# A two-layer hybrid trunk: twelve held expert units with a place each, other PSUM banks for value products and the last scan levels, and the first expert product inside the second gather half

## The reference

```python
def hier_moe(h, wg, bg, we, be, w1, w3, w2):     # 32 experts, 4 groups of 8, 2 experts per token
    gprob = softmax(t @ wg + bg); gidx = top-1 group
    eprob = softmax(logits of that group's 8 experts); top-2, renormalised
    gate = weight of each (token, expert), 0 for most
    for e in range(32):
        he = silu(t @ w1[e]) * (t @ w3[e])
        y = y + gate[:, e:e+1] * (he @ w2[e])
x = x + even_mixer(rmsnorm(x)); x = x + hier_moe(rmsnorm(x))     # layer 0
x = x + odd_mixer(rmsnorm(x));  x = x + hier_moe(rmsnorm(x))     # layer 1
```

## Time and profile before

| what | value |
|---|---|
| runs | 1302.06 us median (1301.33, 1302.06, 1309.36) |
| profiled execution | 1305.92 us, span of its core 1304.1 us |
| PE busy | 1143.5 us (88% of the span), of which the modelled ends are a part |
| DVE, ACT busy | 359.7 us (28%), 217.0 us (17%) |
| DMA | 459.10 MB, mean 352 GB/s |
| granted TensorE clock, mean | 0.973 of full speed |

### The profile page before, as it was taken

How to read it: one execution, slowest core, us unless ns; L and a number is a source line. 1 busy time by engine, 2 the same in 40 slices (tenths; PEclk the granted TensorE clock), 3 DMA queues, 4 the chain that set the end, 5 groups by cost and what they waited for, 6 DMA issues and landing times.

```text
span 1304.1 us, 21374 instructions
## 1 busy us (share of the span) xinstructions
PE 1143.5 (88%) x9133; PEld 644.0 (49%) x9133; DVE 359.7 (28%) x987; ACT 217.0 (17%) x435; POOL 18.3 (1%) x20
## 2 busy tenths in 40 slices
PE   7998899999886878877999999999999787888777
PEld 5665564544433424342787775464554343434332
DVE  4793441111111101011746643241111110101111
ACT  1313221100100000000324453030100010000000
POOL 0121000000000000000000000000000000000000
PEclk9998999999999989999999999999999998998998
DMA  9910399999999999999944446569999999999996
GB/s 387 384 67 1 122 401 419 426 412 429 428 430 428 427 430 428 428 427 428 427 181 162 161 153 233 228 239 428 427 411 431 427 428 431 427 428 429 430 426 273
DMA packets 33791, 459.10 MB, mean 352 GB/s; under 512 B 3760, under 2 KB 3920, under 8 KB 6096
## 3 DMA queue, kind: packets, MB, share of 16 engines
q1 hardware_dynamic: 32544, 454.19, 83.2%
q10 hardware_dynamic: 1200, 4.23, 0.9%
HBM read 457.32 MB, written 1.08 MB: 352 GB/s over the span
## 4 chain that ended last, share of the span: by engine, by line
PE 46%; DMA 41%; DVE 4%; issue 1%; ACT 1%; SPq 0%; DVEq 0%
DMA extra<-in_moe_units 41%; PE bank L752 9%; PE bank L663 8%; PE bank L693 7%; PE bank L683 5%; PE bank L854 4%; PE bank L593 2%; PE bank L642 2%; PE bank L429 1%; PE bank L559 1%; PE bank L653 1%; PE bank L811 1%; PE bank L623 1%; PE bank L617 1%; PE bank L671 0%
## 5 line engine op out<-in xcount | busy, mean ns | idle before, releaser
L693 PE MATMUL bank<-hT,pgT 128*128 128x512 f32 x512 | 244.2, 621 | 0.0
L663 PE MATMUL bank<-ring,xT 128*32 128x256 f32 x2560 | 169.6, 407 | 40.5 <-DMA ring<-in_moe_units 39.7
L693 PEld LDWEIGHTS bank<-hT,pgT 128*128 128x128 f32 x512 | 95.6, 198 | 137.7 <-issue 120.8
L663 PEld LDWEIGHTS bank<-ring,xT 128*32 128x32 f32 x2560 | 83.0, 112 | 122.2 <-DMA ring<-in_moe_units 63.7
L663 PE MATMUL bank<-extra,xT 128*32 128x256 f32 x1536 | 103.2, 412 | 34.7 <-DMA extra<-in_moe_units 34.7
L752 PE MATMUL bank<-h,ring 128*128 128x256 f32 x576 | 130.1, 382 | 0.0
L1495 DVE TENSOR_TENSOR he<-sg,bank 128x128 f32<-128x128 f32 x64 | 18.4, 287 | 400.7 <-ACT sg L1017 400.7
L752 PEld LDWEIGHTS bank<-h,ring 128*128 128x128 f32 x576 | 107.4, 190 | 16.5 <-issue 3.0
L663 PEld LDWEIGHTS bank<-extra,xT 128*32 128x32 f32 x1536 | 52.1, 113 | 92.0 <-DMA extra<-in_moe_units 53.9
L1023 ACT ACTIVATE hT<-bank 128x512 f32<-128x512 f32 x64 | 38.2, 598 | 305.7 <-PE bank L683 305.7
L683 PE MATMUL bank<-extra,heT 128*32 128x512 f32 x512 | 66.0, 634 | 20.8 <-DMA extra<-in_moe_units 11.4
(11 more groups left out here) (290 smaller groups left out, 892.8 us busy)
## 6 DMA issues: line engine op xcount, KB each, us to landing
ring<-in_moe_units SPq DMA_DIRECT2D x112, 2048.0 KB, 32.9
extra<-in_moe_units SPq DMA_DIRECT2D x80, 2048.0 KB, 25.7
ring<-in_od_in_units SPq DMA_DIRECT2D x10, 2048.0 KB, 35.4
ring<-in_ev_in_units SPq DMA_DIRECT2D x5, 2048.0 KB, 29.0
ring<-in_od_out_units SPq DMA_DIRECT2D x4, 2048.0 KB, 7.9
ring<-in_ev_out_units SPq DMA_DIRECT2D x2, 2048.0 KB, 24.2
hT<-sums ACTq DMA_DIRECT2D x4, 512.0 KB, 4.0
every<-sums ACTq DMA_DIRECT2D x4, 512.0 KB, 5.9
```

What stands on the lines that cost most here:

```text
L663: last = mm(bank[4 + e % 2][32 * j:32 * j + 32, 0:256], xT[:, 4 * part + k, CAP * e:CAP * e + CAP], w[:, k, :, 256 * (j // 2) + j % 2:256 ...
L693: last = mm(bank[2 * t + h][:, :], pgT[:, e, t, :], ys[:, e % 2, 512 * h:512 * h + 512], start=False, stop=closed)
```

## The change

Layout: `extra4` is a fifth extra place; it lies over `kk`, `lb_`, `bb` and two constants of the even mixer (`adm`, `cs`), and over `rsb`, `dg` of the odd one. To make room, expert scratch goes into the free half of `hT` and into `pgT`, `ys`, `he`, `heT` and `sg` have one buffer instead of two, `xd[1]` moves onto `extra3`, and the mask of the odd mixer is built by three DVE instructions instead of being loaded. The constants come in two loads, 384 words a row fewer. So twelve units have a place each; `NEXT`, `SHARED` and `SECOND` go, and the loop over `ORDER` starts at step 0, behind SP's wait for `rt_ok` and its read of the step count.

Even mixer: value products write bank 6 instead of 4, and levels 6 and 8 bank 2 (and 3) instead of 0 (and 1). Score b+1 waits for the maximum of score b instead of `at_o`; turn b waits for `at_o` b-1; levels 6 to 8 wait for one level's copy less.

Expert layer: the fourth `fold` product comes after the ranks and replaces the `turnover` there. In step 0, `up(0, 0)` comes after half of the second gather half.

```diff
-RING, EXTRA = 7, 4
+RING, EXTRA = 7, 5
-          (1, 0): RING, (1, 1): RING + 1, (3, 2): RING + 1, (1, 2): RING + 2, (3, 1): RING + 3}
+          (1, 0): RING, (1, 1): RING + 1, (1, 2): RING + 2, (3, 1): RING + 4, (3, 2): RING + 3}
+LEVEL_BANK = (0, 0, 0, 0, 0, 0, 2, 0, 2)
...
-            sp.dma_start(con[:, :], A["con"]).then_inc(in_con, 16)
+            sp.dma_start(con[:, :], A["con"][:, 0:C_KEEP]).then_inc(in_con, 16)
+            sp.dma_start(extra4[:, 3072:3072 + C_END - C_KEEP], A["con"][:, C_KEEP:C_END]).then_inc(in_con, 16)
...
-                for step, (e, part) in NEXT:
-
-                    if (e, part) in SECOND:
-                        sp.wait_ge(used[layer], step * STEP_UNITS + finished(*SHARED[e, part]))
-                    else:
-                        sp.wait_ge(used[layer], finished(*SHARED.get((e, part), (e, part))))
-                    moe_unit(layer, e, part, step * GROUP + e)
                 sp.wait_ge(rt_ok, layer + 1)
                 last_step = sp.value_load(rounds[0:1, 2 + layer:3 + layer], min_val=NGROUPS - 1, max_val=ROUNDS * NGROUPS - 1)
-                with sp.Fori(1, last_step) as i:
+                with sp.Fori(0, last_step) as i:
                     for e, part in ORDER:
...
+                        sp.wait_ge(used[layer], i * STEP_UNITS + finished(e, part))
...
                 if b:
-                    pe.wait_ge(at_o, b)
+                    pe.wait_ge(at_max, b)
...
             def turn(b):
                 pe.wait_ge(at_exp, b + 1)
+                if b:
+                    pe.wait_ge(at_o, b)
...
-                        last = mm(bank[4][:, 64 * m:64 * m + 64], pT[:, P * j:P * j + P], av[:, s_, 64 * (h // 4):64 * (h // 4) + 64],
+                        last = mm(bank[6][:, 64 * m:64 * m + 64], pT[:, P * j:P * j + P], av[:, s_, 64 * (h // 4):64 * (h // 4) + 64],
...
-                    pe.wait_ge(lv_ok, v)
+                    if v == 6:
+                        pe.wait_ge(e_half, 4)
+                    pe.wait_ge(lv_ok, v if v < 6 else v - 1)
...
-                turnover(7, 4)
+                pe.wait_ge(lg_ok, 2 * layer + 2)
+                keep_x(0).then_inc(fold, 1)
...
                     if begin:
-                        gather(0); gather(1)
+                        gather(0); gather(1, (0, 1))
                         pe.wait_ge(m["xt_ok"], i * 2 + 1)
                         up(0, 0)
+                        gather(1, (2, 3))
                         gates(0); gates(1)
...
+            tt(mask3[:, 0:P], strict, ident, ALU.add)
+            v_.memset(mask3[:, P:2 * P], 1.0)
+            ch.put(tt(mask3[:, 2 * P:3 * P], strict, ident, ALU.add))
```

More of the change, by code:

```diff
@@ L618, in moe, with keep_x @@
                 last.then_inc(rt_ps, 1)
-                for a in (1, 2, 3, 0):
-                    if a == 0:
-                        pe.wait_ge(lg_ok, 2 * layer + 2)
-                    last = mm(bank[a][:, :], ident, x[:, a // 2, 512 * (a % 2):512 * (a % 2) + 512], start=True, stop=False)
-                last.then_inc(fold, 1)
+                def keep_x(a):
+                    return mm(bank[a][:, :], ident, x[:, a // 2, 512 * (a % 2):512 * (a % 2) + 512], start=True, stop=False)
+                for a in (1, 2, 3):
+                    keep_x(a)
                 pe.wait_ge(rt_sel, layer + 1)
@@ L1237, in _ @@
             dve.wait_ge(rw_ok, 1)
[L1238 removed]
+            dve.wait_ge(in_con, 48)
             for t in range(NT):
```

187 lines of the change are left out of this document (88 added, 99 removed).

## The result

The changed kernel takes 1291.37 us median (1291.12, 1293.24, 1290.95, 1291.62); the kernel before, in the same comparison, 1305.22 (1302.06, 1301.33, 1309.36, 1308.39). The ratio is 0.9905, 95% interval 0.9881 to 0.9930. The two profiled executions are 14.8 us apart: span 1289.3 against 1304.1, time 1291.12 against 1305.92.

The account below looks back on a forecast made before the run. It took the unbroken stream of expert units (4.895 us each) to bound the kernel. Terms 8.0 + 0.45 + 2.6 + 2.2 made 13.3 us: 1292.6 from the profiled 1305.92, 1288.7 from the median 1302.06; range 1282 to 1297.

Parts of the forecast that it names:

- What bounds the kernel: Expert layers end when their last unit lands; a cut before layer 0's first extra loads arrives whole at the kernel's end.
- The banks: Even mixer, value 0 to final sum: new banks and waits save 8.0 us, ends 5.1 and 8.9.
- The four waits: Even mixer: TensorE's waits for VectorE before scores 1 and 2 and levels 6 and 7, together 5.8 us, all go.
- the clock's 3.1: Even mixer: work after the two long waits runs at the lower clock, costing 3.1 us, which would be saved.
- The first rival: Even mixer: VectorE and ScalarE are met at every level, so the result is 2.9 us worse, 1291.6; chance 0.17.
- The start: Kernel start: 0.20 MB fewer constants bring the units TensorE waits for earlier, saving 0.45 us.
- Layer 0: First expert layer's stream: a break of 1.1 instead of 2.4 us, and no dip at 278; saves 2.6 us.
- the row: SP's reload: 1.25 us for the `rounds` read with loop entry, from the profile, kept over the skill page's 600 ns floor.
- Layer 1: Second expert layer: stream starts 4.0 us later, but one unit less (4.9) and no dip at 954 (1.3); saves 2.2 us.
- Costed at nothing: Single buffers, later gate transposes, odd mixer's mask instructions (0 to 0.7 us) and SP's `pr_ps` wait in layer 1 add nothing.
- Places and orders: The two expert layers' streams, with the twelfth place and new orders: 2.6 us in layer 0 and 2.2 in layer 1.
- the two milder rivals: Mixer paced by VectorE's and ScalarE's lists, 1291.6, chance 0.17; late reload behind `rt_ok` in expert layers, 1292.2, chance 0.16.

Follow-up runs that it names:

- the banks undone: The changed kernel with the even mixer's banks and waits as they were before, everything else still changed: 1300.61 us, ratio 0.9975.
- the banks alone: The kernel before with only the new banks and waits of the even mixer: 1294.91 us, ratio 0.9937.
- the whole gather: The changed kernel with both gather halves ahead of the first expert product in step 0, as before: 1287.82 us, ratio 0.9874.
- the free reloads: The changed kernel with step 1's twelve reloads issued ahead of SP's wait for the step count, the loop starting at step 1: 1287.39 us, ratio 0.9879.
- the fold product back: The changed kernel with both gather halves before the first expert product, plus the fourth fold product ahead of the ranks and idle-filling products behind: 1288.37 us, ratio 0.9874.
- with eleven: The changed kernel with eleven unit places again: 1300.69 us, ratio 0.9975; with both gather halves also ahead of the first expert product: 1294.68 us, ratio 0.9943.
- one half undone: The changed kernel with value products back in bank 4 and scores behind `at_o`, the levels' new banks kept: 1296.35 us, one execution.
- second product ahead of the gates: Against the kernel with step 1's reloads ahead of the step count: up(0, 1) before the gate transposes, warming products started sooner; 1287.91 us, ratio 0.9885.

## Why the prediction was right, and where not

**What bounds the kernel.** Right. What the first extra loads moved arrived at the end (the banks undone and the banks alone, 8.2 to 9.1 us in the times for 8.8 in the queue). What the first reload of layer 1 moved arrived where the queue was empty (2.1 of 2.2 with the whole gather), and in part where it was not (2.9 of 4.8 with the free reloads). The stretches in which the DMA engines are full are 27 of the 40 slices, two thirds of the span and not half; no term hangs on it.

**The banks.** Forecast 8.0, measured 8.8. The four waits and the clock's 3.1 went as said; turn 2 was short by 0.47 as said, but level 7 met its operand in time, which is half of the 0.8 that I was low. The products that I priced with 3.43 against 2.02 are one level (16 instructions in both rows) and not two; the price is right. The first rival (the lists set the pace) had no part.

**The start.** Forecast 0.45, measured 0.1. The term took 0.20 MB less as 0.46 us earlier at TensorE. The unit came only 0.13 and 0.25 earlier in the two kernels in which TensorE was there to meet it, and in the change's execution TensorE was not: the warming products wait for VectorE's first scaling now and start 0.47 later, and the first projection takes 9.97 us instead of the 8.91 of the kernel before, so it ends 1.5 later. I had placed a few tenths of delay inside the DMA wait; this used the wait up. Why the projection took longer is open: in the kernel with the free reloads, with the same start, it took 9.14.

**Layer 0.** Forecast 2.6, measured 2.9 (3.7 up to the step before the end). The dip at 278 went. The reload went out at 187.84, 196.66 on the clock of before, against 197.2 forecast, and 1.22 us after `rounds`, against 1.25. The break was 0.6 us, against 1.1. The gather began 1.5 us sooner after the first extra loads than before, not 0.9, since the eight fold products had run at the low clock before (5.38 us against 3.68 for the same eight in the kernel with the fold product back). That is near the upper end that I gave for it, 1.8, and in part luck: with the whole gather six of the same products ran at the low clock in their new place.

The Trainium skill ("DMA: Bandwidth & Descriptors", Latency and other measured facts) gives a `tensor_load` a floor of about 600 ns. The trace of the change has the read by itself (TENSOR_LOAD at L382): 468 ns in layer 0 and 282 ns in layer 1, below the page's figure. SP's reload followed the ready count by 1.22 and 1.02 us all the same, since the bounds check and the entry to the loop stand between the read and the issue. So the row was the right price to keep.

**Layer 1.** Forecast 2.2, measured 2.7. The reload was forecast at 874.1 on the clock of before and went out at 874.11 (862.40 + 852.88 - 841.17). "The twelfth place alone would have given 4.9; most of it goes to `rt_ok`" is what the free reloads show: without `rt_ok` the reload leaves 4.8 us earlier and 2.9 us of it come through in this layer. The split gather's 2.0 us in that sum is right too (2.2 measured).

**Costed at nothing.** The single buffers, the mask and the `pr_ps` wait: no sign of any. The gate transposes 2 us later: with twelve places TensorE's lead covers it (the split gather costs nothing in layer 0 and in layer 1 the 2.1 us by which the reload is late), with eleven it costs 2.8 and 1.0 us, near the 2 us a layer that the prediction gave as the price without the lead.

**The sum and its anchor.** Places and orders had 4.8 of the sum; by the distances to the layers' ends they are 5.6, of 7 to 9 for the twelfth place less 2 to 4 for the split gather. All terms gave 13.3 and the two profiled executions differ by 14.8. From the profiled time the forecast would be 1292.6, and the measured median is 1291.37. What put the forecast at 1288.7, 2.7 too low, is the last step: I took off the 3.9 us by which the profiled execution of before lay above its median, but the changed kernel's profiled execution lies on its own median (1291.12 against 1291.37). With one more run of before the median of before is 1305.22, next to the profiled one, and the gain from there is 13.9 us, by the ratio 12.4 (9.1 to 15.5). So what missed is the anchor: the sum itself is borne out within what the runs can tell.

**The chances.** 1291.37 lies in the range, within 1% by the median of three and at 0.95% by the ratio. I had the two milder rivals at 1291.6 and 1292.2; the number is near theirs, but for the reason above and not for theirs. In the sum the start, 0.35 too high, hides a part of what the other three terms were too low, 0.3 to 0.8 each.

**What stays open.** Why the kernel before scatters over 8 us (1301 to 1309) and the changed one over 2. The low clock at a layer's end is one source, 1.6 us a layer, and both kernels have it at the end of layer 1 in their profiles. Why the last twelve units of a layer take up to 1.6 us longer than 58.7. And how much of the gap between the split and the whole gather in the times is the gather and how much the place where the clock fell.

## What to carry over

A wait for a buffer that blocks TensorE's in-order list can cost more than its length, since the granted clock can fall behind it: here 5.8 us of waits cost 8.8. A place more in a prefetch pool pays what a unit takes (here 7 to 9 us over two layers, with the dips), but only as far as nothing new stands ahead of the reload on the issuing queue: peel the iterations that always run ahead of a run-time count. And an edit that fills one engine's time (the first expert product early) has to be traced through the other engine's list: here VectorE's copy stood ahead of the count, and the change is faster without that edit (1287.8 us against 1291.4; 2.1 us of it are seen in the traces) and with the reloads freed (1287.4; 3.4 us seen). The two are alternatives, not a sum.

## What the runs showed of the hardware

- The granted clock at the end of a layer is full or low from kernel to kernel though the waits there are alike (1.1 us before the last product in the change and in the kernel with the free reloads): the last w2 product and scatter take 7.2 us in the one and 5.6 in the other. In the kernel with both halves of the banks undone a wait of 1.67 us brought the clock to 1.2 GHz, in the kernel with one half undone the same wait at the same place did not.
- SP's issue of a 2 MB load takes 0.33 us with up to eight others outstanding and mostly about 4 us with nine or more, counted over the 192 expert loads of the change by their issue and landing times; the rate stays at 428 GB/s. In the change 108 issues meet nine or more, in the kernel before 21. The median from issue to landing rose from 32.9 and 25.7 us (ring and extra) to 47.5 and 48.1. A queue that is issued so deep ties SP down: nothing else may be wanted of it.
- 0.20 MB less of constants ahead of a unit brought it 0.13 us (second product ahead of the gates) and 0.25 us (free reloads) earlier, not 0.46, with one load more ahead of it.
- SP's read of one word from SBUF (TENSOR_LOAD) took 0.28 to 0.48 us, four reads in the kernel before and the change.
